# Turning values and second-pass operands by halves of 64 rows in TensorE's two row halves, in an input projection

## The reference, cut to what matters

```python
for layer in range(DEPTH):
    h = rms_norm(x, norm_g[layer])
    if layer % 2 == 0:
        u = h @ w_in_even[i]
        aq, ak, av, ag, bq, bk, bv, bg = jnp.split(u, even_splits, axis=-1)
        ...
    else:
        u = h @ w_in_odd[i]
        cq, ck, cv, cg = jnp.split(u, 4, axis=-1)
        ...
    x = x + y
return rms_norm(x, final_g)
```

## Time and profile before

| | |
|---|---|
| Time, median of 3 runs | 2621.16 us (2620.06 to 2622.87) |
| The profiled execution, its time | 2625.82 us |
| Its span | 2624.0 us |
| Mean granted TensorE clock | 0.972 |
| TensorE busy | 2404.9 us, 92% |
| DVE busy | 1530.9 us, 58% |
| ACT busy | 1152.5 us, 44% |
| POOL busy | 1067.4 us, 41% |

### The profile page before, as it was taken

How to read it: one execution, slowest core, us unless ns; L and a number is a source line. 1 busy time by engine, 2 the same in 40 slices (tenths; PEclk the granted TensorE clock), 3 DMA queues, 4 the chain that set the end, 5 groups by cost and what they waited for, 6 DMA issues and landing times. The chain is left out here.

```text
span 2624.0 us, 44696 instructions
## 1 busy us (share of the span) xinstructions
PE 2404.9 (92%) x16952; PEld 2011.6 (77%) x16952; DVE 1530.9 (58%) x2877; ACT 1152.5 (44%) x2464; POOL 1067.4 (41%) x838
## 2 busy tenths in 40 slices
PE   4999999996999998989979999899998899998998
PEld 4777778875877876768867888778886788887887
DVE  6434565435887795755644432754323688887555
ACT  4333343333777775722233333433332566665221
POOL 5677768771000002310047887778875200100000
PEclk8999999998999999989989999999999899999999
DMA  2555434457464133565524453435433554453352
GB/s 104 166 190 177 149 119 150 150 163 169 104 141 91 45 124 82 164 226 205 208 97 162 160 144 102 139 134 173 133 101 97 189 164 152 142 179 114 146 207 81
DMA packets 221364, 376.67 MB, mean 144 GB/s; under 512 B 54964, under 2 KB 108896, under 8 KB 220128
## 3 DMA queue, kind: packets, MB, share of 16 engines
q1 hardware_dynamic: 200816, 299.35, 35.7%
q0 software_dynamic: 18992, 72.36, 9.3%
q10 hardware_dynamic: 1344, 2.10, 0.2%
HBM read 236.33 MB, written 142.90 MB: 145 GB/s over the span
## 5 line engine op out<-in xcount | busy, mean ns | idle before, releaser
L1052 PE MATMUL p_acc<-p_operands,p_w_hi 128*128 128x512 f32 x1600 | 611.7, 393 | 8.9 <-DVE p_full_out L911 8.6
L291 POOL TENSOR_TENSOR p_w_lo<-p_w_raw,p_w_hi 128x512 fp32r<-128x512 f32 x240 | 333.1, 1397 | 160.0 <-ACT p_w_hi L543 159.7
L1052 PE MATMUL p_acc<-share,p_w_hi 128*128 128x512 f32 x1024 | 384.4, 396 | 10.0 <-DVE p_full_out L911 6.7
L1052 PEld LDWEIGHTS p_acc<-p_operands,p_w_hi 128*128 128x128 f32 x1600 | 302.4, 190 | 71.6 <-POOL p_w_raw L309 4.7
L1052 PE MATMUL p_acc<-share,p_w_lo 128*128 128x512 f32 x896 | 350.6, 391 | 0.0
L543 ACT ACTIVATE p_w_hi<-p_w_raw 128x512 fp32r<-128x512 f32 x252 | 156.5, 624 | 249.3 <-POOL p_w_raw L309 105.3
L1052 PE MATMUL p_acc<-share_low,p_w_hi 128*128 128x512 f32 x624 | 247.9, 397 | 6.2 <-DVE p_operands L698 3.2
L1052 PE MATMUL p_acc<-share_low,p_w_lo 128*128 128x512 f32 x624 | 244.2, 391 | 0.0
L1052 PEld LDWEIGHTS p_acc<-share,p_w_hi 128*128 128x128 f32 x1024 | 192.2, 189 | 51.6 <-DVE p_operands L698 5.9
L831 DVE SCALAR_TENSOR_TENSOR p_lo_out<-p_full_out,p_hi_out 128x512 fp32r<-128x512 f32 x116 | 123.0, 1061 | 184.6 <-ACT p_hi_out L557 184.6
L1822 DVE CUSTOM_DVE_ANT_0 c_prob<-c_logits,c_bias 128x640 f32<-128x640 f32 (+4 forms) x256 | 179.5, 739 | 67.9 <-PE c_logits L1737 50.4
(11 more groups left out here) (248 smaller groups left out, 4867.2 us busy)
## 6 DMA issues: line engine op xcount, KB each, us to landing
scr_qh<-p_hi_out SPq DMA_DIRECT2D x116, 256.0 KB, 2.5
scr_ql<-p_lo_out SPq DMA_DIRECT2D x116, 256.0 KB, 2.7
p_w_raw<-in_w_in_even POOLq DMA_DIRECT2D x26, 1024.0 KB, 7.5
scr_gt<-p_hi_out SPq DMA_DIRECT2D x128, 128.0 KB, 2.0
ready_w<-in_w_in_odd POOLq DMA_DIRECT2D x16, 1024.0 KB, 7.1
p_w_raw<-in_w_in_odd POOLq DMA_DIRECT2D x16, 1024.0 KB, 6.8
share<-scr_qh SPq DMA_DIRECT2D x28, 512.0 KB, 8.4
share<-scr_ql SPq DMA_DIRECT2D x28, 512.0 KB, 9.7
```

What stands on the lines that cost most here:

```text
L291: nc.gpsimd.tensor_tensor(w_lo[:, k, :, :], w_source(e, k), w_hi[:, k, :, :].bitcast(F32), ALU.subtract).then_inc(w_made, 1)
L1052: last = nc.tensor.matmul(bank[:, :], wt[:, k, c, :], at[k][:, c, :], start=starts and step == 0, stop=step == 3 * HK - 1, skip_group_chec ...
```

## The change

Values, and operands of the second pass, are turned by halves. Each transpose of 128x128 becomes two of 64 rows by 128 columns, one in each row half of TensorE, which write into two different PSUM banks. `turned` becomes one tensor of two banks and `acc` one of six, and a group now takes both banks of a pair: its upper rows go to the first bank, its lower rows to the second. Four consequences are in the diff: ACT and DVE read with a pattern that puts the halves of 64 side by side again; for the second pass both tiles of a call are in one pair of banks, so ACT and DVE wait for the later of the two; the value group `i` waits for ACT's copy of `i - 1`, where it waited for `i - 2`; and three of the late operands move to a pair of `acc` banks, with waits to fit. The operands of the first pass are turned as before.

```diff
-        turned = [st.ps(f"turned{i}", [P, HK, P]) for i in range(2)]
-        acc = [st.ps(f"acc{i}", [P, HT]) for i in range(6)]
+        turned = st.ps("turned", [P, 2, HT])
+        acc_ps = st.ps("acc", [P, 6, HT])
+        acc = [acc_ps[:, i, :] for i in range(6)]
...
+        APART = (S1, S3, S4)
...
         def bank_of(q, o):
...
+            return (turned[:, 0, :], turned[:, 1, :], acc[4], acc[5])[turn_at(q, o) % 4]
+
+        def two_banks(q, o):
+            late = q // 2 % 2
+            if late == 0 and o in (S2, A12, A22, S4):
+                first = (4 * LAST + (0 if o == S4 else 4)) % 6
+                return acc_ps[:, first:first + 2, :]
+            if late == 1 and o in APART:
+                first = (4 * NEXT + 4) % 6
+                return acc_ps[:, first:first + 2, :]
+            return turned
+
+        def halves_in(q, o):
+            side = q % 2
+            return two_banks(q, o)[:, :, side * HK * HD:(side + 1) * HK * HD].rearrange("p r (c t) -> p c r t", t=HD)
...
             def high(q, o):
                 if q >= PAIRS:
                     act.wait_ge(mm_done, 7 * LAST + o + 1)
-                act.wait_ge(x_turned, turn_at(q, o) + 1)
+                act.wait_ge(x_turned, turn_at(q if q < PAIRS else q // 2 * 2 + 1, o) + 1)
...
+                    nc.scalar.activation(by_halves(a_hi[o][:, :, tokens_of(q)]), halves_in(q, o), ACT.Copy).then_inc(cast, 1)
...
                 if kind == "v":
                     act.wait_ge(v_turned, v_index[n] + 1)
-                    nc.scalar.activation(hi_out[:, buf, :].bitcast(F32), turned[v_index[n] % 2][:, :, :].rearrange("p t c -> p (t c)"), ACT.Copy).then_inc(act_done, 1)
+                    nc.scalar.activation(hi_out[:, buf, :].bitcast(F32).rearrange("p (t r c) -> p t r c", r=2, c=HD), turned[:, :, 0:TPB * HD].rearrange("p r (t c) -> p t r c", c=HD), ACT.Copy).then_inc(act_done, 1)
...
             def low(q, o):
-                dve.wait_ge(cast, turn_at(q, o) + 1)
+                dve.wait_ge(cast, turn_at(q if q < PAIRS else q // 2 * 2 + 1, o) + 1)
...
                 for c in range(HK):
-                    last = nc.tensor.transpose(bank[:, c, :], source[:, c * P:(c + 1) * P], keep["ident"][:, :])
...
+                    for r in range(2):
+                        rows = slice(r * HD, (r + 1) * HD)
+                        last = nc.tensor.transpose(halves_in(q, o)[:, c, r, :], source[rows, c * P:(c + 1) * P], keep["ident"][rows, rows])
...
             def turn_late(o):
-                before_o = turn_at(PAIRS + 1, S3) if o == A11 else turn_at(PAIRS + 3, o - 1)
-                pe.wait_ge(split, before_o + 1)
+                if o == S1:
+                    pe.wait_ge(taken, 6 * LAST + 6)
+                else:
+                    pe.wait_ge(split, {A11: turn_at(PAIRS + 1, S3), S2: turn_at(PAIRS + 3, A11)}.get(o, turn_at(PAIRS + 3, max(o - 2, 0))) + 1)
...
             def turn_values(n):
                 i = v_index[n]
                 pe.wait_ge(taken, taken_at(n))
-                if i % V >= 2:
-                    pe.wait_ge(act_done, vs[i - 2] + 1)
+                if i % V >= 1:
+                    pe.wait_ge(act_done, vs[i - 1] + 1)
...
                 for t in range(TPB):
-                    last = nc.tensor.transpose(turned[i % 2][:, t, :], full_out[:, n % 2, t * P:(t + 1) * P], keep["ident"][:, :])
+                    for r in range(2):
+                        rows = slice(r * HD, (r + 1) * HD)
+                        last = nc.tensor.transpose(turned[:, r, t * HD:(t + 1) * HD], full_out[rows, n % 2, t * P:(t + 1) * P], keep["ident"][rows, rows])
...
             def product(e, k):
...
+                if k == 0 and e == NEXT + 1:
+                    pe.wait_ge(split, turn_at(PAIRS + 3, S4) + 1)
```

More of the change, by code:

```diff
@@ L230, in bank_of, with by_halves @@
         def bank_of(q, o):
[L231 to L242, removed]
+            return (turned[:, 0, :], turned[:, 1, :], acc[4], acc[5])[turn_at(q, o) % 4]
[11 more added lines that the diff above has]
+            return two_banks(q, o)[:, :, side * HK * HD:(side + 1) * HK * HD].rearrange("p r (c t) -> p c r t", t=HD)
+        def by_halves(whole):
+            return whole.rearrange("p c (r t) -> p c r t", t=HD)
         def tokens_of(q):
@@ L523, in high @@
                     act.wait_ge(mm_done, 7 * LAST + o + 1)
-                act.wait_ge(x_turned, turn_at(q, o) + 1)
-                nc.scalar.activation(a_hi[o][:, :, tokens_of(q)], bank_of(q, o)[:, :, :], ACT.Copy).then_inc(cast, 1)
+                act.wait_ge(x_turned, turn_at(q if q < PAIRS else q // 2 * 2 + 1, o) + 1)
+                if q < PAIRS:
+                    nc.scalar.activation(a_hi[o][:, :, tokens_of(q)], bank_of(q, o).rearrange("p (c t) -> p c t", t=P), ACT.Copy).then_inc(cast, 1)
+                else:
+                    nc.scalar.activation(by_halves(a_hi[o][:, :, tokens_of(q)]), halves_in(q, o), ACT.Copy).then_inc(cast, 1)
             def high_early(o):
@@ L696, in low @@
             def low(q, o):
-                dve.wait_ge(cast, turn_at(q, o) + 1)
-                nc.vector.tensor_tensor(a_lo[o][:, :, tokens_of(q)], bank_of(q, o)[:, :, :], a_hi[o][:, :, tokens_of(q)].bitcast(F32), ALU.subtract).then_inc(split, 1)
+                own, high = a_lo[o][:, :, tokens_of(q)], a_hi[o][:, :, tokens_of(q)].bitcast(F32)
+                dve.wait_ge(cast, turn_at(q if q < PAIRS else q // 2 * 2 + 1, o) + 1)
+                if q < PAIRS:
+                    nc.vector.tensor_tensor(own, bank_of(q, o).rearrange("p (c t) -> p c t", t=P), high, ALU.subtract).then_inc(split, 1)
+                else:
+                    nc.vector.tensor_tensor(by_halves(own), halves_in(q, o), by_halves(high), ALU.subtract).then_inc(split, 1)
             def low_early(o):
@@ L964, in turn @@
                     pe.wait_ge(split, at - 3)
-                bank, source = bank_of(q, o), operand_of(q, o)
+                source = operand_of(q, o)
                 for c in range(HK):
-                    last = nc.tensor.transpose(bank[:, c, :], source[:, c * P:(c + 1) * P], keep["ident"][:, :])
+                    if q < PAIRS:
+                        last = nc.tensor.transpose(bank_of(q, o)[:, c * P:(c + 1) * P], source[:, c * P:(c + 1) * P], keep["ident"][:, :])
+                        continue
+                    for r in range(2):
+                        rows = slice(r * HD, (r + 1) * HD)
+                        last = nc.tensor.transpose(halves_in(q, o)[:, c, r, :], source[rows, c * P:(c + 1) * P], keep["ident"][rows, rows])
                 last.then_inc(x_turned, 1)
```

## The result

The median went from 2620.61 us (2619.99 to 2622.87, 4 runs beside it) to 2644.92 us (2644.28 to 2649.87, 4 runs): a ratio of 1.0096, 95% interval 1.0084 to 1.0108, or +24.3 us. The forecast was +17.3 us, 2638.5. The direction was right, the size was 7 us too small, and the time lies 1.4 us above the range.

What follows compares the result with a forecast made beforehand. TensorE, busy 92% of the span, was taken to bound the kernel. Waits 8.0, value groups 6.1, clock 1.6 and operands 1.6 sum to 17.3 us; 2621.2 + 17.3 = 2638.5 us, range 2618 to 2643.5.

Steps and rivals of the forecast that it cites:

- A value group, 0.15: Input projections: a group alone takes 0.82 us by halves against 0.67 whole, +0.15 each; 6.1 us in all.
- the two bounds for the change of shape: TensorE, 128x128 against 64x128: lower, changing rows costs nothing; upper, it costs what attention's shape changes show, both directions.
- The new waits, 8.0 for four: First value slab of each pass: a group waits for ACT's late copy; 3.4 + 1.8 + 1.7 + 1.1 = 8.0 us.
- The clock, 1.6: After the new wait of 3.4: eight matmuls at the lower granted clock, 0.43 instead of 0.23, +1.6 us (0 to 2.8).
- Copies with halves side by side at nothing: ACT's copies putting halves side by side: no slower per element and under products, so no cost.
- Operands, 1.6: Second-pass operands in slabs LAST and NEXT: -0.5, +2.0 and +0.1, together +1.6 us.
- 10 x 0.20 = +2.0: Slab NEXT: five late operands a layer start ACT 0.20 us later, as it waits for both tiles; +2.0 us.
- The run of A22 and A11 in LAST: Slab LAST: this operand run, with a wait for a split between the two, put at +0.1 us.
- Rows free: Rival: changes of rows cost nothing, waits as forecast; sum -2.6 us, 2618.6, no change that can be told; 12%.
- rows free with copies in time: Rival listed second: row changes free and ACT's copy in time; -13.6 us, 2607.6, faster; 5%.
- one direction only: Rival: only one direction of the shape change costs; operands -1.7, waits and clock near +8.5; about 2628, slower; 7%.
- Waits hidden: Rival: row changes cost as forecast but the new waits are hidden; +9.4 us, 2630.6, slower; 7%.

Runs made afterwards that it cites:

- e3: Kernel before with one idle 64-row half transpose added ahead of the four whole ones of each value group: 2641.6 us, ratio 1.0071.
- e4: Kernel before with one whole 128-row transpose added ahead of each value group, so no change of shape: 2630.05 us, ratio 1.0031.
- e5: Kernel after with ACT's copies of values moved ahead of the rounding of weights that waits for POOL: 2640.94 us, ratio 1.0073.
- e8: Kernel before with only the new wait, each value group waiting for ACT's copy of the group just before; transposes whole: 2633.76 us, ratio 1.0044.
- e11: Kernel after run once more with no edit: 2647.9 us, ratio 1.0097.
- e2: Kernel after with values turned whole again, two banks in turn and the old wait; only second-pass operands by halves: 2629.5 us, ratio 1.0031.
- e6: Kernel after with the two tiles of late operands in NEXT kept in separate pairs of banks, ACT and DVE waiting for their own: 2640.4 us, 1.0074.
- e12: Kernel before with always-met waits added in the projections, 812 more instructions in TensorE's queue and no added work: 2624.12 us, ratio 1.0011.
- e1: Kernel before with only the values turned by halves, second-pass operands still whole: 2638.81 us, ratio 1.0063.

## Why the prediction was wrong, point by point

- **TensorE bounds these stages: right.** What its queue got longer by was paid in full: 39 groups alone add 0.147 each by product ends.
- **A value group, 0.15: right to 0.003.** 0.82 from end to end; start 0.07 ahead, pairs 0.46, 0.07 back, matmul 0.50. The loads, 0.08 before the end ahead, show that they don't lie under it. (The prediction sets the 0.50 against the 0.39 of a matmul within a run; behind whole transposes it took 0.48, so the cost of the way back lies in the later start, not in that duration. The sum goes from end to end and isn't touched.) Of the two bounds for the change of shape the upper one held, in both directions (e3 against e4).
- **The new waits, 8.0 for four: right.** Four waits with ACT as releaser, at the four places, each 0.1 to 0.2 shorter than forecast (6.5 us for 7.1); none other with ACT as releaser among value groups. Waits and clock together, the 39 groups taken off, came to 9.3 for 9.6. e5 takes them away, e8 makes them without the halves.
- **The clock, 1.6: right in the profiled execution, and in part by luck.** One stretch at the lower level behind the wait at 160, 3.4 us long, some 1.5 us of loss; none behind the shorter waits. In e11, the same program, it lasted 6.8 us and cost 1 us more, in e8 too. Waits, groups and clock came to 15.0 for 15.7, and to 16.4 in e11.
- **Copies with halves side by side at nothing: right.** ACT's group, kernel after, 582 ns against 583 in the earlier trace rows:

```profile
L564 ACT ACTIVATE p_hi_out<-p_turned 128x512 f32<-128x512 f32 x52 | 30.3, 582 | 0.3 <-PE p_turned L1042 0.3
```

- **Operands, 1.6: the step that failed.** The LAST runs gave -0.46 for -0.5. The term "10 x 0.20 = +2.0" was mis-sized: it came to 6.3. Per steady link ACT's part is the 0.20, but the link grew by 0.70, since the prediction priced only ACT's wait for both tiles and put DVE's at nothing, without a reason. In the diff, `low` waits in the same way for both of ACT's copies, and the earlier trace rows show these two copies as one run of 1.09 us; DVE's own row, which starts in the middle of it, was not among the rows that the prediction used. Eight steady links of 0.60 to 0.73 make 5.5, the first two links of both layers 0.8, of which 0.6 is the clock stretch at 1717 (in e11 the first links make 0.2). The run of A22 and A11 in LAST, "at +0.1", came to 1.2 by the same wait: PE's idle time ahead of A11 is 1.91 us in layer 1, where it was 0.99. All of it: -0.5 + 1.2 + 6.3 = 7.0, near the 7.2 of the product ends. With 7.2 in place of 1.6 the prediction's own sum gives 22.9 us and 2644.1, which is above its range and 0.8 below the median. e2 measures the part alone (+8.5), e6 gives most of it back. By the Trainium skill, PSUM — Partial Sum Buffer, section PSUM bank collisions raise a hardware error, ScalarE and VectorE may not read one bank in the same partitions at the same time; by that rule DVE's wait for ACT's second copy could not be dropped while the tiles share banks. No run here shows it; e6 moves one tile to other banks.
- **A rest of 2 to 4 us was not foreseen.** e12 makes it likely that gaps without a releaser in layer 1's attention are part of it, and part may be stretches at the lower clock that come and go between executions. Between these it stays open.
- **Rivals.** Rows free, rows free with copies in time, and one direction only: refuted by e3 and e4. A pair of halves is nearly twice as fast as a whole transpose, as the second rival has it, but a group of four is slower, 0.82 against 0.67. Waits hidden: refuted by the four rows above.
- **The range** reached 5 us above the forecast for a longer clock stretch or one more wait. In the profiled execution neither came (in e11 the longer stretch did); what came was a wait repeated in every link of two chains, 5.4 us above its term in all.

## What to carry to other kernels

When two tiles are put into one pair of banks, every consumer behind them becomes serial, not only the first: follow the wait through ACT, DVE and back to TensorE, and multiply by the links of the chain. Transposes by halves can pay in a stage that is in that shape already, where a pair takes 0.062 us against 0.11 for a whole one (no run here tries that); between matmuls of 128 rows a group of four is too short, since it saves 0.2 us in the pairs and pays 0.35 for the two changes of shape, at which the load no longer lies under other work. A buffer that turns from two in turn into one pair needs its release looked up in the consumer's queue: here the copy stood behind a rounding that waited for POOL.

## What the runs showed of the hardware

- A change between 128x128 and 64x128 costs the overlap of the stationary load on both sides: the next start is 0.07 us before the end ahead, not 0.16 to 0.24, and the load starts with it instead of under the matmul ahead. There and back is 0.24 us more than one added whole transpose costs.
- ACT reads halves from two banks and puts them side by side in 582 ns for 512 columns, the same as a plain copy.
- In layer 1's attention TensorE shows gaps of up to 2.2 us without a releaser; at the longest the data queue filled 98.5% of the DMA engines. 812 added instructions that never wait cost 2.9 us (0.3 to 5.2), none of it in the slabs of layer 1's projection, where more than half of them stand.
- In or behind the wait of 3.2 to 3.4 us at 160 the granted clock fell to 0.50 in every trace that has this wait, for 3.4 us (after, e1, e6) or 6.8 us (e8, e11). Gaps of 1.7 to 2.2 us in the attention were followed by a stretch of 3.4 us in e1 (at 2315), e4 (2164) and e5 (2224), and not by one in e11.
